# Seven products for a fourth k-pair per gate/up turn, and the low parts of four units formed by an accumulating DMA

## The reference, cut to what matters

```python
def swiglu(h, wg, wu, wd):
    return (jax.nn.silu(h @ wg) * (h @ wu)) @ wd

x = x + 0.5 * swiglu(rmsnorm(x, g_ffn1), w1_gate, w1_up, w1_down)
...
x = x + 0.5 * swiglu(rmsnorm(x, g_ffn2), w2_gate, w2_up, w2_down)
x = x + sigmoid(rmsnorm(x, g_ple) @ w_ple_gate) * (p @ w_ple_proj)
```

## Time and profile before

| | us |
|---|---|
| median of three runs | 2433.75 (2433.02 to 2434.05) |
| span of the profiled execution | 2432.5 |
| PE busy | 2417.7 |
| DVE busy | 1765.8 |
| ACT busy | 1309.0 |
| POOL busy | 0.4 |

### The profile page before, as it was taken

The page is one execution under the profiler, slowest core; times in us unless marked ns, Lnnn a source line. Parts: engine busy times, 40 slices in busy tenths (PEclk is TensorE's granted clock), DMA queues, the critical chain, the costliest instruction groups (busy, mean ns, idle before and its releaser), DMA issues.

```text
span 2432.5 us, 29257 instructions
## 1 busy us (share of the span) xinstructions
PE 2417.7 (99%) x11104; PEld 2009.4 (83%) x11104; DVE 1765.8 (73%) x2136; ACT 1309.0 (54%) x1594; POOL 0.4 (0%) x5
## 2 busy tenths in 40 slices
PE   9999999999999999999999999999999999999999
PEld 7888888878888877888888888888888888878887
DVE  6888989688876665657655455558898987787765
ACT  6555555554555665454454444455555555554553
POOL 0000000000000000000000000000000000000000
PEclk9999999999999999999999999999999999999999
DMA  7665656646656654655634666556565666566654
GB/s 241 195 212 182 214 184 207 199 166 214 191 188 193 182 157 132 196 182 181 191 116 127 200 190 191 189 184 201 184 207 183 205 200 201 180 200 200 206 186 165
DMA packets 192237, 457.54 MB, mean 188 GB/s; under 512 B 14632, under 2 KB 16624, under 8 KB 192112
## 3 DMA queue, kind: packets, MB, share of 16 engines
q1 hardware_dynamic: 191664, 455.52, 58.8%
q10 hardware_dynamic: 448, 0.34, 0.0%
HBM read 453.70 MB, written 2.10 MB: 187 GB/s over the span
## 4 chain that ended last, share of the span: by engine, by line
PE 95%; DVE 4%; ACT 1%; issue 0%; DMA 0%; SPq 0%; ACTq 0%
PE ps L424 37%; PE ps L444 13%; PE ps L446 13%; PE ps L445 13%; PE ps L551 5%; PE ps L553 5%; PE ps L552 5%; PE ps L622 1%; PE ps L454 1%; PE ps L638 1%; DVE wl L1310 1%; PE ps L462 1%; ACT wh L903 1%; PE ps L649 0%; DVE aTl L1471 0%
## 5 line engine op out<-in xcount | busy, mean ns | idle before, releaser
L1310 DVE TENSOR_TENSOR wl<-raw,wh 128x1024 fp32r<-128x1024 f32 x786 | 952.2, 1222 | 566.9 <-ACT wh L903 561.3
L903 ACT ACTIVATE wh<-raw 128x1024 fp32r<-128x1024 f32 x786 | 824.1, 1057 | 815.0 <-PE ps L424 400.1
L444 PE MATMUL ps<-wh,hT 128*128 128x512 f32 x1232 | 483.8, 393 | 2.1 <-DVE hT L1330 1.4
L446 PE MATMUL ps<-wh,hT 128*128 128x512 f32 x1232 | 480.1, 390 | 0.0
L445 PE MATMUL ps<-wl,hT 128*128 128x512 f32 x1232 | 480.0, 390 | 0.0
L424 PE MATMUL ps<-wh,hT 128*128 128x512 f32 (+1 forms) x1536 | 415.0, 388 | 1.2 <-DVE om L1576 1.0
L424 PEld LDWEIGHTS ps<-wh,hT 128*128 128x128 f32 x1536 | 283.6, 188 | 57.5 <-issue 1.2
L444 PEld LDWEIGHTS ps<-wh,hT 128*128 128x128 f32 x1232 | 231.8, 188 | 49.8 <-DVE hT L1330 1.7
L446 PEld LDWEIGHTS ps<-wh,hT 128*128 128x128 f32 x1232 | 231.6, 188 | 48.4
L445 PEld LDWEIGHTS ps<-wl,hT 128*128 128x128 f32 x1232 | 231.9, 188 | 46.7
L424 PE MATMUL ps<-wl,hT 128*128 128x512 f32 (+1 forms) x768 | 234.5, 387 | 0.0
(11 more groups left out here) (277 smaller groups left out, 2790.2 us busy)
## 6 DMA issues: line engine op xcount, KB each, us to landing
raw<-in_w_in SPq DMA_DIRECT2D x208, 512.0 KB, 3.6
raw<-in_w_gate SPq DMA_DIRECT2D x176, 512.0 KB, 3.7
raw<-in_w_up SPq DMA_DIRECT2D x176, 512.0 KB, 4.5
raw<-in_w_down SPq DMA_DIRECT2D x176, 512.0 KB, 4.4
raw<-in_w_o SPq DMA_DIRECT2D x32, 512.0 KB, 4.0
raw<-in_w_ple_gate SPq DMA_DIRECT2D x32, 512.0 KB, 3.5
raw<-in_w_br_mla SPq DMA_DIRECT2D x16, 512.0 KB, 4.8
raw<-in_w_br_dil SPq DMA_DIRECT2D x16, 512.0 KB, 3.7
```

What stands on the lines that cost most here:

```text
L444: pe.matmul(ps[:, b0 + t, :], xh, wh[:, s, c], start=first, stop=False)
L446: mm = pe.matmul(ps[:, b0 + t, :], xl, wh[:, s, c], start=False, stop=last)
L903: act.activation(wh[:, j % SLOTS, :], raw[:, j % SLOTS, :], ACT.Copy).then_inc(hi_ready, 1)
L1310: dve.tensor_tensor(wl[:, j % SLOTS, :], raw[:, j % SLOTS, :], wh[:, j % SLOTS, :].bitcast(F32), ALU.subtract).then_inc(lo_ready, 1)
```

## The change

It does four things, in the turns 1 to 9 of both FFNs:

1. `FAST_PAIRS` is (1, 2, 4, 5): four of eight pairs take seven products. The forms of the activations (`FH`, `FL`, `whole_x`, `forms`) get a fourth pair and new places; `FL` becomes two tensors.
2. The odd (up) unit of each of the four plain pairs 0, 3, 6 and 7 (v = 1, 7, 13, 15) gets its low part in another way: ACT writes `wh`, then writes the negated rounded copy into `wl`, and GpSimd issues a DMA that adds the unit's 512 KB from HBM onto `wl`. PE waits for that DMA (`sum_in`), SP's next load into the raw slot for ACT's copies (`hi_ready`), and `lo_ready` no longer counts these units (`lows`).
3. PE fires `front_done` when it has read the first halves of `TH` and `TL`; ACT's copy of the first half of the next sums waits for that, and only the second half for `fast_done`.
4. POOL's list gets the 72 DMAs.

```diff
-        FAST_TURNS, FAST_PAIRS = range(1, FFN_TURNS - 1), (1, 3, 5)
+        FAST_TURNS, FAST_PAIRS = range(1, FFN_TURNS - 1), (1, 2, 4, 5)
...
+        def by_dma(n):
+
+            if not isinstance(n, int):
+                return False
+            n -= U_GU2 if n >= U_GU2 else U_GU1
+            m, v = divmod(n, FFN_BODY)
+            return m in FAST_TURNS and v % 2 == 1 and v // 2 not in FAST_PAIRS
+
+        def lows(n):
+
+            return n - (sum(by_dma(i) for i in range(n)) if isinstance(n, int) else TURN_DMAS)
+
+        def sums_in(n):
+
+            return sum(by_dma(i) and i % SLOTS == n % SLOTS for i in range(n + 1))
...
                 if waits and not (isinstance(n, int) and n < SLOTS):
-                    sp.wait_ge(lo_ready, n + waits - SLOTS)
+                    if by_dma(n - SLOTS):
+                        sp.wait_ge(hi_ready, n - SLOTS + 1)
+                    else:
+                        sp.wait_ge(lo_ready, lows(n + waits - SLOTS))
...
+            def low_parts(u0, w_gate, w_up):
+                for m in FAST_TURNS:
+                    for v in range(FFN_BODY):
+                        n, k, c0 = u0 + m * FFN_BODY + v, v // 2 * 2, m * BANK
+                        if by_dma(n):
+                            pool.wait_ge(hi_ready, n + 1)
+                            pool.dma_start(wl[:, n % SLOTS, :].rearrange("p (k c) -> p k c", k=2),
+                                           (w_gate, w_up)[v % 2][0, k * P:(k + 2) * P, c0:c0 + BANK]
+                                           .rearrange("(k p) c -> p k c", p=P), accum_op=ALU.add)\
+                                .then_inc(sum_in[n % SLOTS // 2], 16)
...
-                pe.wait_ge(lo_ready, n + 1)
+                if by_dma(n):
+                    pe.wait_ge(sum_in[n % SLOTS // 2], 16 * sums_in(n))
+                else:
+                    pe.wait_ge(lo_ready, lows(n + 1))
...
                 product(b1 + 2, S3, T3, first, last)
-                product(b1 + 3, S1, T1, first, last)
+                product(b1 + 3, S1, T1, first, last).then_inc(front_done, 1)
...
-                act.activation(wh[:, j % SLOTS, :], raw[:, j % SLOTS, :], ACT.Copy).then_inc(hi_ready, 1)
+                high = act.activation(wh[:, j % SLOTS, :], raw[:, j % SLOTS, :], ACT.Copy)
+                if by_dma(n):
+                    high = act.activation(wl[:, j % SLOTS, :], raw[:, j % SLOTS, :], ACT.Copy, scale=-1.0)
+                high.then_inc(hi_ready, 1)
...
-                    if count and a == 0:
-                        act.wait_ge(fast_done, count)
+                    if count:
+                        act.wait_ge((front_done, fast_done)[a], count)
...
+                if by_dma(n):
+                    return
                 dve.wait_ge(hi_ready, n + 1)
```

More of the change, by code:

```diff
@@ L136, in hybrid_layer @@
         aR = at("aR", 44 * KB, [P, KF, S])
-        FH, FL = at("FH", 0, [P, 4, 3, P], F32R), at("FL", 6 * KB, [P, 4, 3, P], F32R)
+        FH = at("FH", 0, [P, 4, 4, P], F32R)
+        FL = [at(f"FL{a}", where * KB, [P, 2, 4, P], F32R) for a, where in enumerate((8, 84))]
         sums, ends = at("sums", 12 * KB, [P, 4, BANK]), at("ends", 20 * KB, [P, 4, BANK])
         TH, TL = at("TH", 28 * KB, [P, 4, BANK], F32R), at("TL", 36 * KB, [P, 4, BANK], F32R)
-        whole_x, forms = at("whole_x", 28 * KB, [P, 3, 2, S]), at("forms", 36 * KB, [P, 4, 3, P])
+        whole_x, forms = at("whole_x", 28 * KB, [P, 4, 2, S]), at("forms", 36 * KB, [P, 4, 4, P])
         TH_d, TL_d = whole("TH_d", 16 * KB, [P, 4, BANK], F32R), whole("TL_d", 24 * KB, [P, 4, BANK], F32R)
@@ L189, in hybrid_layer @@
         unit_done = sem("unit_done")
+        sum_in = [sem(f"sum_in{a}") for a in range(2)]
         x_first, x_in = sem("x_first"), [sem(f"x_in{j}") for j in range(4)]
@@ L198, in hybrid_layer @@
             sem(n) for n in ("sig_ready", "am_ready", "a_turned", "a_raw", "ah_ready", "a_ready"))
-        forms_raw, forms_hi, forms_ready, sums_ready, TH_ready, TL_ready, fast_done, p1_out, g1_free, ends_ready, ups_out, a_forms_raw, a_forms_hi, a_forms_ready, g1_out = (
-            sem(n) for n in ("forms_raw", "forms_hi", "forms_ready", "sums_ready", "TH_ready", "TL_ready", "fast_done",
+        forms_raw, forms_hi, forms_ready, sums_ready, TH_ready, TL_ready, front_done, fast_done, p1_out, g1_free, ends_ready, ups_out, a_forms_raw, a_forms_hi, a_forms_ready, g1_out = (
+            sem(n) for n in ("forms_raw", "forms_hi", "forms_ready", "sums_ready", "TH_ready", "TL_ready", "front_done", "fast_done",
                              "p1_out", "g1_free", "ends_ready", "ups_out", "a_forms_raw", "a_forms_hi", "a_forms_ready", "g1_out"))
@@ L535, in fast_turn @@
                         q = FAST_PAIRS.index(p)
-                        forms = [(FH[:, a, q, :], FL[:, a, q, :]) for a in range(4)]
+                        forms = [(FH[:, a, q, :], FL[a // 2][:, a % 2, q, :]) for a in range(4)]
                         fast_pair(u + 2 * p, 2 * p, p, hTh, hTl, forms, TH, TL, q == 0, q == len(FAST_PAIRS) - 1,
@@ L1385, in make_forms @@
                 if step == 0:
-                    chain(dve.tensor_tensor(whole_x[:, :, :, :], hi, lo, ALU.add))
+                    both = whole_x[:, :, :, :].rearrange("p (q r) k s -> p q (r k) s", q=2)
+                    chain(dve.tensor_tensor(both, hi, lo, ALU.add))
                 if step == 1:
@@ L1395, in make_forms @@
                     dve.wait_ge(forms_hi, f + 1)
-                    dve.tensor_tensor(FL[:, :, :, :], forms[:, :, :, :], FH[:, :, :, :].bitcast(F32), ALU.subtract)\
-                       .then_inc(forms_ready, 1)
+                    for a in range(2):
+                        low = dve.tensor_tensor(FL[a][:, :, :, :], forms[:, 2 * a:2 * a + 2, :, :],
+                                                FH[:, 2 * a:2 * a + 2, :, :].bitcast(F32), ALU.subtract)
+                    low.then_inc(forms_ready, 1)
             def half_split(n, j):
```

15 lines of the change are left out of this document (9 added, 6 removed).

## The result

| | us |
|---|---|
| before, median | 2433.68 (2433.02 to 2434.05) |
| changed, median of four runs | 2732.31 (2728.57 to 2737.72) |
| ratio | 1.1232 (95% interval 1.1218 to 1.1246) |

The changed kernel is slower by 298.6 us. The sign and the kind of cause were forecast, the size was not: the forecast was 143 us more, less than half of it.

A forecast was written before the change was run, and what follows sets the result against it. PE's matmul count was taken to bound the kernel. With the change, chain B at L = 7.3 makes a turn 50.3 us against 42.33: 8.0 x 18 turns = 143 us more, 2577 us, range 2490 to 2740.

The forecast's parts named there:

- chain A: Fast turn without accumulating DMA, through DVE's work, raw-slot release, loads and ACT's copies: 45.7 us a turn.
- What bounds the kernel now: Fast turns before the change: PE's matmul count sets the time, 42.28 us; ACT's and DVE's chain stays hidden.
- What the change removes: One more fast pair per turn saves 54 matmuls, 12.2 us; alone that would give 2421.5 us.
- Busy times: Work per fast turn after the change: DVE 37.1 us as before, ACT 30 of 42; neither over the turn.
- cheap DMA: Rival: L under 5, chain A decides, 45.7 us a turn, 2494 us; chance 0.14.
- B: Fast-turn chain from unit 7 through unit 13 and DVE's pair 2 back: 35.7 + 2 L, 50.3 us a turn.
- C: Fast-turn chain from unit 7 to 13, 1 and 7 by slots and `TH` alone: 28.0 + 3 L, 49.9 us.
- L: Time from ACT's second copy of a DMA-fed unit to PE's start on it: 7.3 us, between 5.0 and 10.5.
- dear DMA: Rival: L over 10.5, chain C decides, over 59.5 us a turn, 2743 us and more; chance 0.10.
- The gain arrives: Rival: PE's count still sets the time with chains hidden, 2421.5 us; chance 0.05.
- near zero: Rival: cheap DMA and chain A at 42.3 us, eating just the gain; chance 0.03.
- The signs named beforehand: Fast turns of 48 to 55 us, PE idle ahead of units 1, 7, 13, DMAs landing after 6 to 8 us.

The follow-up runs named there:

- e1_no_dma: The changed kernel with POOL's accumulating DMAs left out, PE waiting for ACT's copies instead; 2494.71 us, 1.025 against the kernel before.
- e6_filled_gaps: The changed kernel with PE running 16 and 20 zero matmuls ahead of its waits at units 7 and 13; 2673.5 us, 1.0982 against the kernel before.
- the best version: Four fast pairs, DVE doing all low parts, no DMA, `gs` later and the turn-end bank copy and adds earlier; 2469.48 us, 1.0156 against the kernel before.

## Why the prediction was right and wrong

The four levels of time, all measured, name what each part costs when they are added in this order:

| | us | step |
|---|---|---|
| before | 2433.7 | |
| four fast pairs without the DMA (`e1_no_dma`) | 2494.7 | + 61.0: chain A, with the gain of 12.2 inside |
| with the DMA, gaps filled (`e6_filled_gaps`) | 2673.5 | + 178.8: waits for the DMA at full clock |
| the change | 2732.3 | + 58.8: half clock after the gaps |

- **What bounds the kernel now**: right. PE's count and pitch held, and the chains of ACT and DVE were hidden only by the turn's length.
- **What the change removes**: right as a count; the 12.2 us never came to light, since PE's count no longer bounds the turn.
- **Busy times**: right. DVE 37.36 a turn (37.1 forecast), ACT 29.41 (30).
- **Chain A**: right to 0.5 us (46.0 to 46.2 and 45.8 to 45.9 against 45.7), and leg by leg in `e1_no_dma`. The kernel's time came out at 0.7 and 4 us from the 2494; the 0.7 is in part luck, since the turns themselves were 0.3 to 0.5 us longer than forecast. Repaired, it gave 44.60. These kernels are the rival "cheap DMA" made real; the changed kernel is not.
- **Chains B and C**: C is the right mechanism, and every leg of it but L and the slow matmuls came within 0.3 us. B, on which the forecast of 50.3 us rests, set no turn that was read: above L = 7.7 it is C, and where L was 6 it was a chain through L only once, which the prediction does not have.
- **"The size of L"** is the step that failed. The 7.3 us was put together from a second pass at load speed (1.24), a load ahead in the queue (1.24) and 1 us for software. No row stood behind the 1 us. Measured were 8.15, 8.56 and 9.52 in one turn, 8.7 in the mean. The addition costs 2.8 us over the plain copy, not one pass of 1.24, and POOL's way 1.1 to 1.8. Since C counts L three times, 1.4 us of error became 4.3 in chain C of the turn read above, 3.9 over the forecast turn of 50.3. Over the kernel this term is the 96 us between 2577 and 2673.5, 5.4 a turn, with the L of 9.1 of that run.
- **A term that was missing**: PE's own clock. The profile's page gave its clock as full, and it was put at nothing without a reason; but the forecast itself had gaps ahead of the units 1, 7 and 13, 8.7 us a turn in all (50.3 less PE's 41.6). The slow matmuls behind the gaps cost 58.8 us on top. The 155 us of the miss are these two.
- **The rivals**: of "dear DMA" (2743 us) the picture was right, chain C decides, but not by L over 10.5: at L = 8.7 the half clock brought the turn to its 59. "The gain arrives" and "near zero" had no run near them; the best version stayed 37 us over the kernel before.
- **The signs named beforehand**: PE's idle time ahead of the units 1, 7 and 13 came, released by the DMA. Turns of 48 to 55 us and landings of 6 to 8 us did not: 58.8 and 8.6.
- **"POOL's waits hold nobody else"** and the raw slot's release: right; the loads landed 0.3 and 0.2 us later than before (4.0 and 4.7 against 3.7 and 4.5 in the earlier trace rows), and in chain C none of them appears. Releasing `TH` by halves was put into the chains without a price; it has one, 46 us.

What stays open: what besides the length of an idle time decides whether the clock falls (1.56 us in one kernel did both); why L grew from 8.15 to 9.52 within a turn; whether the same DMA issued while fewer loads run would land sooner; and whether more raw slots would shorten chain A below 41.6, which was not tried.

## What to carry to other kernels

- Before work is moved from a busy engine to a DMA, ask whether that engine's busy time sets the turn at all: here DVE's four low parts could be kept or replaced by ACT's copies alone with no gain (2489.7 and 2494.7 us). The path goes through buffers and their release, and it is found by walking from each buffer's release to its next use.
- Compare the latency of the new transfer with the time from its earliest issue to its use, and count how often one round of the chain goes through it. Three times an error of 1.4 us is more than the whole gain that was sought, 0.7 us a turn.
- An idle TensorE cost twice here: the gap, and the half clock behind it. A forecast that contains such gaps needs a term for the clock; where the gap can't be removed, matmuls that add zero give that part back (58.8 us here).

## What the runs showed of the hardware

- A DMA by GpSimd that adds 512 KB from HBM onto f32 data in SBUF, with the DMA engines 0.65 to 0.69 busy: 8.6 us from issue to landing in the median, 6.3 to 11.0 in all, 1.21 us of issue on POOL, 1.85 times a load's engine time per byte. 256 KB: 5.9 us. Without addition 5.8 us and 0.72 us.
- TensorE's first seven matmuls after an idle time of 4.22 us and the twelve after 5.64 us ran at half clock (pitch 0.43 us); after 1.16 us and 2.50 us the pitch was 0.23 from the second interval on. In `e1_no_dma` an idle time of 1.56 us was followed by seven slow matmuls in one turn, and by none in the turn before it.
- DVE and GpSimd, both with two operands in SBUF, slow each other: DVE from 1.41 to 3.53 us and from 1.22 to 1.95, GpSimd from 2.40 to 4.53.
